# The time mix levels of an RWKV-7 layer: two halves of the chunks half a level apart

## The chip, the cores and the metric

The kernel runs on one core of one Trainium2 chip. It is one launch, and what counts is the device time of that launch in microseconds (us). The core has five engines that run their own instruction queues and meet at semaphores: PE (TensorE, matrix products), DVE (VectorE), ACT (ScalarE), POOL (GpSimd) and SP (SyncE). In the profile PEld stands for the weight loads of PE, which overlap its products. PE writes only to the eight PSUM banks; DVE and ACT read them from there.

## The reference, cut to what matters

The program is a whole model of several layers in float32 on 512 tokens of width 1024. Its first layer is an RWKV-7 time mix with 16 heads of width 64, a recurrence over the tokens:

```python
def rwkv7_time_mix(x, mu, w_rkv, ...):
    ...
    def step(S, inp):
        r_t, d_t, k_t, v_t, a_t, b_t = inp
        sa = jnp.einsum('bhij,bhj->bhi', S, a_t)
        S = (S * d_t[:, :, None, :] + sa[..., None] * b_t[:, :, None, :]
             + v_t[..., None] * k_t[:, :, None, :])
        return S, jnp.einsum('bhij,bhj->bhi', S, r_t)

    _, y = lax.scan(step, state0, tuple(seq_first(z) for z in (r_h, decay, k_h, v_h, vec_a, vec_b)))
    ...
```

What follows (group norm, gate, output product, feed-forward, attention layers, a second block) is not touched by the change and is left out here.

## The kernel before

The heads are taken in pairs (`PAIRS` = 8, index `n`), one head on the first 64 partitions and one on the last 64. The 512 tokens of a pair are cut into 8 chunks of 64. Inside a chunk the recurrence is a lower triangular system, and the kernel inverts its 64x64 matrix by doubling: from 2x2 blocks to 4x4 and so on, in five **levels** (`LEVELS` = 1 to 5). A pair goes through three parts:

1. the opening (`opening_tensor`, `opening_vector`): the products that make the matrices, into PSUM, and their masks. It ends on PE with three dense products of the next pair;
2. the levels (`levels_tensor`, `levels_vector`), which the change rewrites;
3. the scan over the eight chunks (`scan_tensor`, `scan_vector`), which needs the finished inverses, and in which one dense product of the next pair stands behind each short product that has to wait for DVE.

The chunks are in two groups, `g` = 0 (chunks 0 to 3) and `g` = 1 (4 to 7). In a level each chunk and head has three 64x64 products: T (`ga` times `xz[..., 0]`), which DVE multiplies by the mask of the level into `ti`; then X and Z (both with `ti` and `xz[..., 1]`), which DVE adds to `xz`. The last level has no X. `PLACES` says which quarter of the 128x128 array a product uses: T and X use the two quarters off the diagonal (from the rows of one head to the partitions of the other), Z the two on it. Products in different quarters run side by side. Each float32 product shows as two records in the trace.

A level on PE is: T of group 0, T of group 1, a fill, X and Z of group 0, X and Z of group 1, a fill. DVE masks group 0 and then 1, has a fill of its own, and adds group 0 and then 1. A **fill** is work of something else that is written between: on PE, by `in_level`, dense products of the next pair (`dense_tensor`, numbered 3 to 10; 3 to 7 are the last of the keys, at L476; 8 is two short products for w and a, at L491 and L492; 9 and 10 are r, at L498), `var_tensor` (L522) and `spread_tensor` (L530) of the group norm of the pair before; on DVE, by `in_levels`, the rest of that norm (`y_var` to `gated`, L1014 to L1037) and `sigmoid` (L867) of the next pair. In the last pair the fills on PE are output products (L697) instead. The first pair has no norm to finish.

All queues are strictly in the order in which the code writes them. PE waits for `level_dve` (steps of DVE), DVE for `level_pe`; each step is one increment of a semaphore.

Of the kernel before, what the change touches and what calls it, by code (L numbers as in the profile page):

```python
# [18 lines left out]
ALU = mybir.AluOpType  # L19
# [3 lines left out]
P = 128  # L23
T = 512
# [5 lines left out]
CH = 64  # L30
# [202 lines left out]
def refined(dve, v, r, done):  # L233
# [30 lines left out]
LEVEL_PE = ["low", "gram0", "gram1"] + [f"{w}{lv}_{g}" for lv in LEVELS for w in ("T", "XZ") for g in range(2)]  # L264
LEVEL_DVE = (["bonus", "low", "x_first", "gram_b0", "gram_b1", "gram_k0", "z_one0", "z_one1", "z_first", "gram_k1"]
             + [f"{w}{lv}_{g}" for lv in LEVELS for w in ("T", "XZ") for g in range(2)])
# [12 lines left out]
class TimeMix:  # L279
# [321 lines left out]
    def levels_tensor(self, pe, n, fill):  # L601

        ps, S, V = self.k.ps, self.level_pe, self.level_dve
        xz, ti = self.xz, self.ti

        for lv in LEVELS:
            for g in range(2):
                pe.wait_ge(V.sem, V.at(n, f"XZ{lv - 1}_{g}" if lv > 1 else f"gram_b{g}"))  # L610
                for c in range(4):
                    for rows, other in self.PLACES:
                        ins = pe.matmul(ps[other, 2 * g, 256 + c * CH:256 + c * CH + CH], self.ga[rows, 4 * g + c, 0:CH],
                                        xz[rows, g, 0, c, :], start=True, stop=True)
                S.done(ins, f"T{lv}_{g}")
            fill(lv, 0)
            for g in range(2):
                pe.wait_ge(V.sem, V.at(n, f"T{lv}_{g}"))
                if lv == 1 and g:
                    pe.wait_ge(self.turned_act.sem, self.turned_act.at(n, "K"))  # L620
                for c in range(4):
                    cols = slice(c * CH, c * CH + CH)
                    if lv < LEVELS[-1]:
                        for rows, other in self.PLACES:
                            pe.matmul(ps[rows, 2 * g, cols], xz[other, g, 1, c, :], ti[other, 4 * g + c, :], start=True, stop=True)
                    for rows, other in self.PLACES:
                        ins = pe.matmul(ps[other, 2 * g + 1, cols], ti[other, 4 * g + c, :], xz[other, g, 1, c, :], start=True,
                                        stop=True)
                S.done(ins, f"XZ{lv}_{g}")
            fill(lv, 1)  # L630
# [70 lines left out]
    def tensor(self, pe):  # L701
# [10 lines left out]
        in_level = {(1, 0): 1, (1, 1): 1, (2, 0): 1, (2, 1): 1, (3, 0): 1, (4, 1): 1, (5, 0): 2}  # L712
# [248 lines left out]
    def levels_vector(self, dve, n, fill):  # L961
        k, ps, S, V = self.k, self.k.ps, self.level_pe, self.level_dve
        levels = k.const(CR_AT, "levels")
        for lv in LEVELS:
            mask = levels[:, lv * CH:lv * CH + CH].unsqueeze(1).broadcast_to([P, 4, CH])
            for g in range(2):
                dve.wait_ge(S.sem, S.at(n, f"T{lv}_{g}"))
                V.done(dve.tensor_tensor(self.ti[:, 4 * g:4 * g + 4, :], ps[:, 2 * g, 256:512].rearrange("p (c t) -> p c t", c=4),
                                         mask, ALU.mult), f"T{lv}_{g}")
            fill(lv)  # L970
            for g in range(2):
                dve.wait_ge(S.sem, S.at(n, f"XZ{lv}_{g}"))
                if lv < LEVELS[-1]:
                    both = self.xz[:, g].rearrange("p w c t -> p w (c t)")
                    ins = dve.tensor_tensor(both, both, ps[:, 2 * g:2 * g + 2, 0:256], ALU.add)
                else:
                    z = self.xz[:, g, 1].rearrange("p c t -> p (c t)")
                    ins = dve.tensor_tensor(z, z, ps[:, 2 * g + 1, 0:256], ALU.add)
                V.done(ins, f"XZ{lv}_{g}")
# [2297 lines left out]
```

## Time and profile before

| | us |
|---|---|
| median of 3 runs | 2375.32 (2373.02 to 2380.53) |
| the profiled execution | 2380.81 |
| its span in the trace | 2379.0 |
| from the first weight load of the levels to the first of the scan, pair 2 | 21.91 |
| one whole pair (opening, levels, scan) | 60.68 |

The profile lists instructions by engine with start and length; "idle before" is how long the engine stood still, and behind the arrow stands who released it. A timeline merges neighbours of one line into one row (x32 is 32 records). The chain of work is followed back from the last instruction to what released each step. Mean granted clock of PE over the span is 0.98 of full speed, and 1.00 in the time mix up to the last pair's scan.

### The profile page before, as it was taken

The page shows a single profiled execution, that of the slowest core. Times are in us where ns is not written, and L with a number is a line of the kernel's source. Part 1 is how long each engine was busy: PE and PEld are TensorE (multiplying, and loading weights), DVE is VectorE, ACT ScalarE, POOL GpSimd, SP SyncE. Part 2 cuts the span into 40 slices and gives each one's busy share as a digit, 9 for nine tenths or more (in the row PEclk, how much of TensorE's full clock was granted, in tenths as well). Part 3 has the DMA queues.
Part 4 walks back from the last instruction along what each step waited for, and adds up shares of the span by engine and source line. Part 5 has one row for each costly group of instructions (what it writes and reads, how often), then busy time and mean ns, then how long its engine had stood idle before and what let it go on. Part 6 is the DMA issues. An engine that isn't in the chain of part 4 may idle for free.

```text
span 2379.0 us, 38698 instructions
## 1 busy us (share of the span) xinstructions
PE 2281.1 (96%) x15454; PEld 1526.7 (64%) x15454; DVE 1149.0 (48%) x2701; ACT 652.1 (27%) x1461; POOL 5.6 (0%) x9
## 2 busy tenths in 40 slices
PE   7999999998999999999999897999999998999998
PEld 3555555555788888865486776888845554444553
DVE  7455555552766662254336565632553564222542
ACT  2222222211333320145332222301221452113541
POOL 0000000000000000000000000000000000000000
PEclk9999999999999999999999999999899998999998
DMA  2100000002222222211113232222212110221111
GB/s 105 61 32 32 32 32 32 20 20 90 89 89 80 81 99 98 85 33 39 54 54 95 91 103 74 106 98 85 106 53 80 36 45 36 72 72 51 36 36 71
DMA packets 27123, 154.78 MB, mean 65 GB/s; under 512 B 5856, under 2 KB 5984, under 8 KB 13152
## 3 DMA queue, kind: packets, MB, share of 16 engines
q1 hardware_dynamic: 22032, 145.57, 17.1%
q0 software_dynamic: 4944, 7.10, 1.3%
q8 instruction: 110, 1.80, 0.3%
q14 instruction: 37, 0.30, 0.0%
HBM read 146.61 MB, written 6.03 MB: 64 GB/s over the span
## 4 chain that ended last, share of the span: by engine, by line
PE 88%; DMA 5%; DVE 5%; issue 1%; ACT 1%; DVEq 0%; SPq 0%; ACTq 0%
PE banks L1868 14%; PE banks L1329 11%; PE banks L1201 7%; PE banks L1129 6%; DMA arena<-up 5%; PE banks L2358 5%; PE banks L1248 3%; PE banks L2210 3%; PE banks L508 3%; PE banks L476 3%; PE banks L498 2%; PE banks L1171 2%; PE banks L1838 2%; PE banks L2244 2%; PE banks L2222 2%; PE banks L2955 2%
## 5 line engine op out<-in xcount | busy, mean ns | idle before, releaser
L1868 PE MATMUL banks<-arena 128*128 128x256 f32 x2016 | 443.0, 381 | 30.9 <-DMA arena<-up 25.9
L1868 PEld LDWEIGHTS banks<-arena 128*128 128x128 f32 x2016 | 383.5, 191 | 90.9 <-issue 36.4
L1329 PE MATMUL banks<-arena 128*128 128x256 f32 x1232 | 267.5, 378 | 0.0
L1329 PEld LDWEIGHTS banks<-arena 128*128 128x128 f32 x1232 | 232.3, 189 | 33.5
L1201 PE MATMUL banks<-arena 128*128 128x512 f32 x384 | 170.8, 602 | 0.0
L1923 ACT ACTIVATE arena<-banks 128x256 f32<-128x256 f32 x180 | 69.0, 384 | 282.8 <-PE banks L1868 282.8
L2083 DVE SCALAR_TENSOR_TENSOR arena<-arena 128x511 f32<-128x511 f32 (+1 forms) x144 | 108.2, 752 | 68.2 <-ACT arena L1932 51.0
L1129 PE MATMUL banks<-arena 128*128 128x512 f32 x320 | 141.1, 602 | 0.0
L2311 DVE CUSTOM_DVE_ANT_0 arena<-banks,arena 128x256 f32<-128x256 f32 (+3 forms) x160 | 70.8, 472 | 132.7 <-PE banks L2210 132.2
L2279 ACT ACTIVATE arena<-arena 128x128 f32<-128x128 f32 (+3 forms) x192 | 101.5, 530 | 121.9 <-DVE arena L2311 121.8
L2067 DVE TENSOR_TENSOR arena<-arena 128x512 f32<-128x512 f32 x144 | 97.3, 691 | 74.3 <-DMA arena<-up 57.9
L1201 PEld LDWEIGHTS banks<-arena 128*128 128x128 f32 x384 | 72.8, 192 | 93.5 <-issue 91.4
L2358 PE MATMUL banks<-arena 128*128 128x512 f32 x256 | 127.7, 627 | 3.0 <-DVE arena L1786 3.0
L1129 PEld LDWEIGHTS banks<-arena 128*128 128x128 f32 x320 | 61.3, 193 | 77.7 <-issue 77.7
L1447 DVE TENSOR_TENSOR arena<-arena 128x1408 f32<-128x1408 f32 x32 | 51.6, 1625 | 104.8 <-DMA arena<-down 82.3
L2210 PE MATMUL banks<-arena 64*128 64x256 f32 (+7 forms) x384 | 93.7, 451 | 0.9 <-DVE arena L2311 0.9
L2222 PEld LDWEIGHTS banks<-arena 128*128 128x128 f32 x392 | 47.4, 144 | 62.3 <-issue 33.5
L1248 PE MATMUL banks<-arena 128*128 128x256 f32 x384 | 85.8, 379 | 0.0
L2358 PEld LDWEIGHTS banks<-arena 128*128 128x128 f32 x256 | 45.2, 193 | 58.8 <-issue 53.7
L1248 PEld LDWEIGHTS banks<-arena 128*128 128x128 f32 x384 | 71.6, 189 | 9.8
L2222 PE MATMUL banks<-arena 128*128 128x128 f32 x392 | 62.0, 283 | 12.2 <-DVE arena L2328 6.8
L1932 ACT ACTIVATE arena<-arena 128x512 f32<-128x512 f32 x72 | 58.2, 811 | 48.8 <-DVE arena L2075 48.8
(324 smaller groups left out, 3186.3 us busy)
## 6 DMA issues: line engine op xcount, KB each, us to landing
arena<-up SPq DMA_DIRECT2D x44, 1024.0 KB, 4.8
arena<-down SPq DMA_DIRECT2D x16, 1408.0 KB, 6.1
arena<-w_mix SPq DMA_DIRECT2D x8, 1728.0 KB, 7.0
arena<-e_in SPq DMA_DIRECT2D x12, 1024.0 KB, 4.8
arena<-o_in SPq DMA_DIRECT2D x8, 1024.0 KB, 4.8
arena<-w_o SPq DMA_DIRECT2D x4, 1024.0 KB, 4.9
arena<-q SPq DMA_DIRECT2D x8, 512.0 KB, 3.4
arena<-o_attn SPq DMA_DIRECT2D x4, 1024.0 KB, 4.8
```

Of the source, the lines that this page charges most:

```text
L476: ins = pe.matmul(ps[:, 4, :], w(8 + j), self.xk[:, j, :], start=j == 0, stop=j == 7)
L1129: ins = pe.matmul(k.ps[:, j, :], k.ring[s][:, (m * kt + t) * P:(m * kt + t + 1) * P], source[:, t, :], start=t == 0, stop=t == kt - 1)
L1201: ins = pe.matmul(k.ps[:, j % 4, :], ring[:, (m * KT + t) * P:(m * KT + t + 1) * P], k.h[:, t, :], start=t == 0, stop=t == KT - 1)
L1248: return pe.matmul(k.ps[:, first_bank + 2 * s + m, half], k.ring[s][:, (m * KT + t) * P:(m * KT + t + 1) * P], bridge.xg[n][:, t, half], s ...
L1329: ins = pe.matmul(ps[:, bank, LO], w[:, t, :], x[:, t, :], start=first and t == 0, stop=t == last, skip_group_check=not first)
L1868: ins = pe.matmul(out, w[:, q, :], x[:, q, :], start=start and q == 0, stop=q == 3, skip_group_check=not start)
L2067: W.done(dve.tensor_tensor(self.s[name], x, y, op), name)
L2083: dve.scalar_tensor_tensor(conv[m][:, shift:T], self.row[m][:, 0:T - shift], self.k.vec("conv", col + tap), conv[m][:, shift:T], ALU.mult, ...
L2210: self.scored.done(pe.matmul(self.k.ps[:, w, 0:k1 - k0], part.query(n, w, b), part.key(n, w, k0, k1), start=True, stop=True), "x")
L2222: ins = pe.transpose(self.k.ps[:, bank, o:o + P], p[:, i * P:i * P + P], self.ident)
L2279: self.exped.done(act.activation(p, raw, ACT.Exp, bias=self.col("max", c, w), scale=-1.0, accum_out=self.col("sum", c, w)), "x")
L2358: ins = pe.matmul(k.ps[:, 6 + n % 2, :], k.ring[slot][:, t * P:t * P + P], k.h[:, t, :], start=t == 0, stop=t == KT - 1)
```

## The change

Three things are done, all in the levels.

**The stretches.** Before the first level PE computes T of group 0 alone (`first`). Then each level has a stretch A: T of group 1 together with Z and X of group 0, chunk by chunk; a fill; and a stretch B: T of group 0 for the next level together with Z and X of group 1; a fill. One step of `level_pe` is signalled at the end of each stretch, where before each group had its own. DVE does, behind A, the mask of group 1 and the sum of group 0, and behind B, the mask of group 0 for the next level and the sum of group 1. In the last level there is no X, and B has Z alone.

**The fills on PE.** `in_level` had one dense product at each of (1,0), (1,1), (2,0), (2,1), (3,0), (4,1) and two at (5,0). Now there is one at each of (1,1), (2,0), (2,1), (3,0), (4,0), (4,1), (5,0), (5,1). The sum stays 8. `var_tensor` stays at (1,0) and `spread_tensor` at (3,1).

**The fills on DVE.** `y_var`, `y_inverse`, `y_r0` go from level 1 to 2, and `y_r1` to `y_r3` from 2 to 3.

```diff
-            for g in range(2):
-                pe.wait_ge(V.sem, V.at(n, f"XZ{lv - 1}_{g}" if lv > 1 else f"gram_b{g}"))
-                for c in range(4):
-                    for rows, other in self.PLACES:
-                        ins = pe.matmul(ps[other, 2 * g, 256 + c * CH:256 + c * CH + CH], self.ga[rows, 4 * g + c, 0:CH],
-                                        xz[rows, g, 0, c, :], start=True, stop=True)
-                S.done(ins, f"T{lv}_{g}")
+            pe.wait_ge(V.sem, V.at(n, f"T{lv}_0"))
+            pe.wait_ge(V.sem, V.at(n, f"XZ{lv - 1}_1" if lv > 1 else "gram_b1"))
+            for c in range(4):
+                below(1, c)
+                ins = inverse(lv, 0, c)
+            S.done(ins, f"A{lv}")
             fill(lv, 0)
...
+            pe.wait_ge(V.sem, V.at(n, f"XZ{lv}_0"))
+            if lv == 1:
+                pe.wait_ge(self.turned_act.sem, self.turned_act.at(n, "K"))
+            for c in range(4):
+                if lv < LEVELS[-1]:
+                    below(0, c)
+                ins = inverse(lv, 1, c)
+            S.done(ins, f"B{lv}")
             fill(lv, 1)
...
-        in_level = {(1, 0): 1, (1, 1): 1, (2, 0): 1, (2, 1): 1, (3, 0): 1, (4, 1): 1, (5, 0): 2}
+        in_level = {(1, 1): 1, (2, 0): 1, (2, 1): 1, (3, 0): 1, (4, 0): 1, (4, 1): 1, (5, 0): 1, (5, 1): 1}
...
+        dve.wait_ge(S.sem, S.at(n, "first"))
+        masked(1, 0)
         for lv in LEVELS:
...
+            dve.wait_ge(S.sem, S.at(n, f"A{lv}"))
+            masked(lv, 1)
+            added(lv, 0)
             fill(lv)
...
+            dve.wait_ge(S.sem, S.at(n, f"B{lv}"))
+            if lv < LEVELS[-1]:
+                masked(lv + 1, 0)
+            added(lv, 1)
...
-        in_levels = {1: ["y_var", "y_inverse", "y_r0"], 2: ["y_r1", "y_r2", "y_r3"], 4: ["normed"], 5: ["biased", "gated"]}
+        in_levels = {2: ["y_var", "y_inverse", "y_r0"], 3: ["y_r1", "y_r2", "y_r3"], 4: ["normed"], 5: ["biased", "gated"]}
```

`below` is the product T and `inverse` the products Z and X, with the same operands as before.

PE, first pair, from the last dense product of the opening on. Before (L613 is T, L625 is X, L627 is Z, L476 a dense product):

```order
L476 MATMUL banks<-arena 128x512 x2
L613 MATMUL banks<-arena 64x64 [waits mix_level_dve]
L613 MATMUL banks<-arena 64x64 x7
L613 MATMUL banks<-arena 64x64 [waits mix_level_dve]
L613 MATMUL banks<-arena 64x64 x7
L476 MATMUL banks<-arena 128x512
L625 MATMUL banks<-arena 64x64 [waits mix_level_dve]
L625 MATMUL banks<-arena 64x64
L627 MATMUL banks<-arena 64x64 x2
```

And in the changed kernel (L611 is T, L618 is Z, L621 is X):

```order
L476 MATMUL banks<-arena 128x512 x2
L611 MATMUL banks<-arena 64x64 [waits mix_level_dve]
L611 MATMUL banks<-arena 64x64 x7
L611 MATMUL banks<-arena 64x64 [waits mix_level_dve]
L611 MATMUL banks<-arena 64x64
L618 MATMUL banks<-arena 64x64 x2
L621 MATMUL banks<-arena 64x64 x2
L611 MATMUL banks<-arena 64x64 x2
L618 MATMUL banks<-arena 64x64 x2
L621 MATMUL banks<-arena 64x64 x2
```

Each half level before had two waits, one for each group, and a dense product behind T; now a stretch has one wait at its start, nothing stands between `first` and A1, and T of one group alternates with Z and X of the other.

DVE, first pair, in the levels. Before (L968 the mask, L975 and L978 the sum, L867 `sigmoid`):

```order
L968 TENSOR_TENSOR arena<-banks,arena 128x256 [waits mix_level_pe] x2
L975 TENSOR_TENSOR arena<-arena,banks 128x512 [waits mix_level_pe] x2
L968 TENSOR_TENSOR arena<-banks,arena 128x256 [waits mix_level_pe] x2
L867 TENSOR_SCALAR arena<-arena 128x512 [waits mix_early_act]
L978 TENSOR_TENSOR arena<-arena,banks 128x256 [waits mix_level_pe] x2
```

And in the changed kernel, the last two levels (L981 the mask, L987 and L990 the sum, L881 `sigmoid`):

```order
L981 TENSOR_TENSOR arena<-banks,arena 128x256 [waits mix_level_pe]
L987 TENSOR_TENSOR arena<-arena,banks 128x512
L981 TENSOR_TENSOR arena<-banks,arena 128x256 [waits mix_level_pe]
L990 TENSOR_TENSOR arena<-arena,banks 128x256
L881 TENSOR_SCALAR arena<-arena 128x512 [waits mix_early_act]
L990 TENSOR_TENSOR arena<-arena,banks 128x256 [waits mix_level_pe]
```

Each DVE instruction of the levels waited for PE before; now one wait stands ahead of a mask and a sum.

## Rows read from the trace of the kernel before

**Rows 1.** The page: busy time by engine, with its share of the span.
```profile
PE 2281.1 (96%) x15454; PEld 1526.7 (64%) x15454; DVE 1149.0 (48%) x2701; ACT 652.1 (27%) x1461; POOL 5.6 (0%) x9
```

**Rows 2.** The chain in order of time (start us, length us, what): pairs 1 and 2.
```profile
141.77 2.78 PE banks L476 x6
...
202.45 2.78 PE banks L476 x6
```

**Rows 3.** Busy time of each engine (us) in the levels of pairs 0, 2 and 7.
```profile
85.29:105.71 20.42, 19.49 (x467) 12.79 (x466) 10.66 (x22) 4.55 (x6) 0.00 (x0) 1.00 0.21 82
...
205.16:227.07 21.91, 21.22 (x491) 14.40 (x490) 13.43 (x31) 4.81 (x7) 0.00 (x0) 1.00 0.20 78
505.95:527.74 21.79, 21.14 (x495) 14.37 (x492) 15.22 (x34) 1.08 (x3) 0.00 (x0) 1.00 0.15 51
```

The columns behind the stretch are its length, then PE, PEld, DVE, ACT and POOL with their records, the granted clock, the DMA share and GB/s.

**Rows 4.** Timeline of PE (start, length, what), pair 2, levels 1 to 3.
```profile
206.24 1.05 PE L522 MATMUL banks<-arena 128*128 128x2 f32 x8
...
210.33 1.15 PE L613 MATMUL banks<-arena 64*64 64x64 f32 x32
211.41 1.12 PE L476 MATMUL banks<-arena 128*128 128x512 f32 x2
212.47 0.27 PE L625 MATMUL banks<-arena 64*64 64x64 f32 x2
...
214.62 1.15 PE L613 MATMUL banks<-arena 64*64 64x64 f32 x32
```

**Rows 5.** Timeline of DVE, pair 2, level 2.
```profile
211.06 0.89 DVE L968 TENSOR_TENSOR arena<-banks,arena 128x256 f32<-128x256 f32 x2 [0.83 <-PE banks L613]
...
213.23 1.28 DVE L975 TENSOR_TENSOR arena<-arena,banks 128x512 f32<-128x512 f32 x2 [0.79 <-PE banks L627]
```

**Rows 6.** Timeline of the weight loads, pair 2, levels 4 and 5 and the scan's first.
```profile
218.86 1.01 PEld L613 LDWEIGHTS banks<-arena 64*64 64x64 f32 x32 [0.17 <-DVE arena L975]
220.07 0.14 PEld L625 LDWEIGHTS banks<-arena 64*64 64x64 f32 x2 [0.20 <-DVE arena L968]
...
222.34 1.01 PEld L613 LDWEIGHTS banks<-arena 64*64 64x64 f32 x32 [0.76 <-DVE arena L975]
...
225.34 0.78 PEld L627 LDWEIGHTS banks<-arena 64*64 64x64 f32 x24 [0.76 <-issue]
...
227.07 0.22 PEld L640 LDWEIGHTS banks<-arena 64*64 64x64 f32 x4 [0.72 <-issue]
```

**Rows 7.** Timeline of DVE, pair 2, levels 4 and 5.
```profile
219.60 0.89 DVE L968 TENSOR_TENSOR arena<-banks,arena 128x256 f32<-128x256 f32 x2 [0.80 <-PE banks L613]
220.40 0.74 DVE L1031 SCALAR_TENSOR_TENSOR arena<-arena,banks 128x512 f32<-128x512 f32 x1
221.06 1.28 DVE L975 TENSOR_TENSOR arena<-arena,banks 128x512 f32<-128x512 f32 x2
...
223.88 0.74 DVE L1034 SCALAR_TENSOR_TENSOR arena<-arena 128x512 f32<-128x512 f32 x1
224.66 0.69 DVE L1037 TENSOR_TENSOR arena<-arena 128x512 f32<-128x512 f32 x1
225.27 0.42 DVE L867 TENSOR_SCALAR arena<-arena 128x512 f32<-128x512 f32 x1
226.07 0.89 DVE L978 TENSOR_TENSOR arena<-arena,banks 128x256 f32<-128x256 f32 x2 [0.38 <-PE banks L627]
```

**Rows 8.** Groups of instructions by line (busy us, mean ns, idle before): sum and mask.
```profile
L975 DVE TENSOR_TENSOR arena<-arena,banks 128x512 f32<-128x512 f32 x64 | 41.1, 685 | 23.8 <-PE banks L627 23.8
...
L968 DVE TENSOR_TENSOR arena<-banks,arena 128x256 f32<-128x256 f32 x80 | 33.9, 425 | 33.8 <-PE banks L613 32.2
```

**Rows 9.** The chain: eight and two dense products in a row.
```profile
65.33 6.88 PE banks L508 x16
...
102.14 1.91 PE banks L498 x4
```

**Rows 10.** Timeline of ACT, pair 2: w of the next pair.
```profile
222.42 0.69 ACT L768 ACTIVATE arena<-banks,arena 128x512 f32<-128x512 f32 x1 [3.08 <-PE banks L492]
```

More of the change, by code:

```diff
@@ L263 @@
              "b", "b_grown", "a_decayed", "rk", "r_decayed"]
[L264 removed]
+LEVEL_PE = ["low", "gram0", "gram1", "first"] + [f"{w}{lv}" for lv in LEVELS for w in "AB"]
 LEVEL_DVE = (["bonus", "low", "x_first", "gram_b0", "gram_b1", "gram_k0", "z_one0", "z_one1", "z_first", "gram_k1"]
[L266 removed]
+             + ["T1_0"] + [x for lv in LEVELS for x in (f"T{lv}_1", f"XZ{lv}_0") + (f"T{lv + 1}_0",) * (lv < 5) + (f"XZ{lv}_1",)])
 SCAN_PE = [f"{w}{c}" for c in range(NC) for w in (("rhs", "u", "side", "state", "y") if c < NC - 1 else ("rhs", "u", "side", "y"))]
@@ new lines, in below, with inverse @@
+        def below(g, c):
+            for rows, other in self.PLACES:
+                ins = pe.matmul(ps[other, 2 * g, 256 + c * CH:256 + c * CH + CH], self.ga[rows, 4 * g + c, 0:CH],
+                                xz[rows, g, 0, c, :], start=True, stop=True)
+            return ins
+        def inverse(lv, g, c):
+            cols = slice(c * CH, c * CH + CH)
+            for rows, other in self.PLACES:
+                ins = pe.matmul(ps[other, 2 * g + 1, cols], ti[other, 4 * g + c, :], xz[other, g, 1, c, :], start=True, stop=True)
+            if lv < LEVELS[-1]:
+                for rows, other in self.PLACES:
+                    ins = pe.matmul(ps[rows, 2 * g, cols], xz[other, g, 1, c, :], ti[other, 4 * g + c, :], start=True, stop=True)
+            return ins
@@ new lines, in levels_tensor @@
+        pe.wait_ge(V.sem, V.at(n, "gram_b0"))
+        for c in range(4):
+            ins = below(0, c)
+        S.done(ins, "first")
+        for lv in LEVELS:
+            pe.wait_ge(V.sem, V.at(n, f"T{lv}_0"))
[4 more added lines that the diff above has]
+            S.done(ins, f"A{lv}")
+            fill(lv, 0)
+            pe.wait_ge(V.sem, V.at(n, f"XZ{lv}_0"))
+            if lv == 1:
+                pe.wait_ge(self.turned_act.sem, self.turned_act.at(n, "K"))
+            for c in range(4):
+                if lv < LEVELS[-1]:
+                    below(0, c)
+                ins = inverse(lv, 1, c)
+            S.done(ins, f"B{lv}")
@@ L963, in levels_vector, with masked, added @@
         levels = k.const(CR_AT, "levels")
-        for lv in LEVELS:
[L965 to L969, printed above, removed]
-            fill(lv)
[L971 to L979, printed above, removed]
+        def masked(lv, g):
+            mask = levels[:, lv * CH:lv * CH + CH].unsqueeze(1).broadcast_to([P, 4, CH])
+            V.done(dve.tensor_tensor(self.ti[:, 4 * g:4 * g + 4, :], ps[:, 2 * g, 256:512].rearrange("p (c t) -> p c t", c=4),
+                                     mask, ALU.mult), f"T{lv}_{g}")
+        def added(lv, g):
+            if lv < LEVELS[-1]:
+                both = self.xz[:, g].rearrange("p w c t -> p w (c t)")
+                ins = dve.tensor_tensor(both, both, ps[:, 2 * g:2 * g + 2, 0:256], ALU.add)
+            else:
+                z = self.xz[:, g, 1].rearrange("p c t -> p (c t)")
+                ins = dve.tensor_tensor(z, z, ps[:, 2 * g + 1, 0:256], ALU.add)
+            V.done(ins, f"XZ{lv}_{g}")
+        dve.wait_ge(S.sem, S.at(n, "first"))
+        masked(1, 0)
+        for lv in LEVELS:
+            dve.wait_ge(S.sem, S.at(n, f"A{lv}"))
+            masked(lv, 1)
+            added(lv, 0)
+            fill(lv)
+            dve.wait_ge(S.sem, S.at(n, f"B{lv}"))
+            if lv < LEVELS[-1]:
+                masked(lv + 1, 0)
+            added(lv, 1)
     def scan_vector(self, dve, n, fill):
```

13 lines of the change are left out of this document (removed).

## The prediction, made before the changed kernel ran

> **What bounds the kernel now.** I read the page first, then the busy time by stretch, then the timelines of PE and DVE through one pair. PE is busy for 96% of the span and DVE for 48% [rows 1], so the question is only how long PE takes for a pair and where it stands still. The chain passes the same point of the opening every 60.68 us [rows 2], and 21.91 us of that are the levels; PE is busy in 21.22 of these [rows 3]. A pair has thus under 1 us of idle PE in its levels, at a granted clock of 1.00, the 2.4 GHz level. That is all that a better order could win without taking work away, some 5.5 us in eight pairs.
>
> How a level hides DVE today is seen in level 2. T takes PE 1.08 us (210.33 to 211.41), the dense product 1.06 us (to 212.47), and X and Z with the next dense product 2.15 us (to 214.62) [rows 4]. DVE starts on the first group 0.73 us after T began [rows 5], long before PE is through with the second group. So what PE needs first, group 0, is made while PE computes group 1. Where no dense product stands between, this shows: in level 4 T begins at 218.86 and X and Z at 220.07, 1.21 us later, after the mask of group 0 alone; PE is idle for about 0.13 us [rows 6]. The other wait is at the end: the last Z begins at 225.34 and the scan at 227.07, 1.73 us for 1.08 us of products [rows 6].
>
> **The round trip of a stretch.** The change signals once per stretch, at its end, and lets DVE do a mask and a sum before PE may start the next stretch, which needs both. The terms:
> - From the start of a stretch to DVE's first instruction. With half of the products it is 0.73 us for T and 0.76 us for X and Z [rows 4, 5]. The second of two masks ends 0.89 us after the first began and takes 0.425 us [rows 5, 8], so it began 0.47 us after the first: it too waited for PE, whose second half takes that long. A whole stretch therefore wakes DVE after 1.20 to 1.23 us. I take 1.22.
> - Mask and sum. Two DVE instructions with no wait between overlap by 0.08 us: L1031 takes 0.74 us, and the next starts 0.66 us behind it [rows 7]. So 0.425 - 0.08 + 0.685 [rows 8] = 1.03 us.
> - From DVE's end to PE's weight load: 219.60 + 0.425 = 220.02, and the load is at 220.07 [rows 6, 7]: 0.05 us.
>
> Together 2.30 us, with a bound of 2.28 below. PE's own work in the same time is 1.09 for the stretch and 1.06 for the dense product, 2.15 us at most [rows 4]; with w and a as the fill 2.27 (220.07 to 222.34) [rows 6]. The round trip ends last in every stretch, by 0.15 us where a dense product fills it. That a mixed stretch is no longer than one of X and Z rests on the quarters: X and Z put 8 products in each of four quarters; T of one group with X and Z of the other puts 8 into the two off the diagonal and 4 into the two on it. No row shows the alternating order. If the swaps of the two off-diagonal quarters cost something, I allow 0 to 0.06 us per stretch, the upper end being about one record's spacing (1.08 us by 16 records in each of two quarters is 0.07) [rows 4]; I take 0, since the order of X and Z with its four quarters costs no more than that of T with two. The bound above is thus 2.36 us.
>
> **A pair, part by part.**
> 1. `first` to A1. Nothing stands between. Half a T wakes DVE after 0.73, the mask takes 0.425, the release 0.05: 1.21 us, of which PE works 0.61. This is the same 1.21 us that level 4 shows now [rows 6].
> 2. A1 to A5 are eight intervals. In a middle pair A1 has the norm's sums as its fill (L522, at most 1.05 us [rows 4]), B3 its spread; both are shorter than the round trip allows. 8 x 2.30 = 18.40 us.
> 3. A5 and B5 have 4 products per quarter, 0.61 us each. On PE: 0.61 + 1.06 (product 9) + 0.61 + 1.06 (product 10) = 3.34 us to the scan. On DVE: 0.75 to wake, 0.34 mask, 0.34 sum of Z (an L978 takes as long as a mask: two of either in 0.89 us [rows 7]), then its fill: `biased` 0.78, `gated` 0.61, `sigmoid` 0.34 [rows 7], and only then the last sum, 0.42 and 0.05 to the scan: 3.63 us. DVE ends last. The wait for w that `sigmoid` has is met: product 8 is ready a whole stretch earlier, and ACT needs 0.69 us [rows 10].
>
> A middle pair: 1.21 + 18.40 + 3.63 = 23.24 us against 21.91, **+1.33 us**, six times: +8.0. The first pair has no norm, so PE ends last: 1.21 + 18.40 + 3.34 = 22.95 us against 20.42 [rows 3]: +2.5; it gains least from the fills, since A1 and B3 now stand bare. The last pair has no `sigmoid`: DVE 3.29, PE 3.34, so 22.95 us against 21.79: +1.2. **Sum: +11.7 us**; with 2.28 us it is 10.4, with 2.36 it is 15.5 (64 intervals).
>
> What the change saves is in there: X, Z and T share stretches, so PE has 0.3 us less of tile work in a pair (10 x 1.085 = 10.85 against 3 x 0.61 + 8 x 1.09 = 10.55), and the late half of level 5 has cover. It is lost to the wait for DVE. The steps of the norm that move on DVE (`y_var` and on) cost nothing: DVE has 2.30 - 1.03 = 1.27 us free in each interval, and they are six short ones. Product 3 moves behind the norm's sums and product 7 a half level on; ACT's copy of the key starts later, and its next reader, product 9, stands two stretches behind. The scan and the opening keep their order, and no DMA issue is moved.
>
> **A rule on the drain.** Eight dense products in a row take 6.88 us, two 1.91 [rows 9], one 1.06 [rows 4]: 0.86 each, and 0.2 per run. The change has two more runs in a middle pair (9 and 10 apart; 3 parted from L522). The Trainium skill (TensorEngine Tiling (Array Packing), Key Properties) says that a change of tiling mode drains the engine, and speaks against such a change; the trace agrees with 0.2 us. By that rule alone the change would cost 0.4 us a pair, some 3 us; by my sum this lies under the round trip and costs nothing of its own.
>
> **Rivals.** (a) The round trip stays hidden and PE sets the pace. It decides where the trip falls to 2.15 us, 0.15 less than my rows give; mask and sum would have to overlap far more than 0.08 us, or DVE wake earlier. Then a middle pair is 1.21 + 8 x 2.15 + 3.34 = 21.75, -0.16; the first pair 21.75, +1.3; the last -0.05; the sum is 0.3 us: 2375.6, not slower. Against it: 1.28 us for two sums and 0.89 for two masks are the same in all eight pairs. Even this best case is no gain, because the start of the levels is bare. For over 0.3% faster each pair would have to lose 0.9 us, all of its idle time. (b) The diagonal quarters don't run beside the alternating pair, so that a stretch has 12 slots in place of 8: +0.47 us each, in 64 intervals +30 us: 2417. It speaks against it that X and Z share the array in 1.09 us. (c) The change doesn't do what it says: what is late is not the round trip but the DVE fill in level 5 alone; then each pair is near (a) plus 0.3 us, 2378. It needs the same short trip as (a).
>
> **How the numbers follow.** The profiled execution of before took 2380.8 us, 5.5 over the median of 2375.3; the levels are all at clock 1.00, so the difference of 11.7 carries over: 2392.5 for an execution like that one, and for the median 2375.3 + 11.7 = **2387.0**. My sum has 0.76; (a) and (c) together 0.17; (b) 0.04; something faster 0.03. The runs of before spread by 3 to 5 us, so the sum's own 2385.7 to 2390.8 becomes 2382 to 2394; I let the lower end reach to 2380 for a part of (c). Under 0.3% (7.1 us) this kernel's measurement can't tell a difference from none: 2368.2 to 2382.4 is "same". Faster 0.04, same 0.20, slower 0.76.
>
> **What would show it.** In the changed profile: starts of stretches 2.28 to 2.36 us apart in all pairs, each released by the DVE sum; DVE's mask 1.2 us behind a stretch's start; 1.21 us from `first` to A1; 3.6 us from A5 to the scan, with L881 just ahead of the last sum; the pair's period 62.0 us in place of 60.68. Wrong would be: stretches 2.15 apart with PE never idle (rival a), a stretch of products longer than 1.15 us (b), or a scan or opening that has changed its length.

## The result

| | us |
|---|---|
| the changed kernel, median of 4 runs | 2398.02 (2391.92 to 2406.84) |
| before, beside it, 4 runs | 2374.17 (2369.88 to 2380.53) |
| ratio, with its 95% interval | 1.0094 (1.0065 to 1.0123) |
| the profiled execution; its span | 2397.51; 2395.7 |

The change made the kernel slower, as forecast, but by about twice the forecast: 22 us or so instead of 11.7, and the median of 2398.0 us lies above the range of 2380 to 2394.

**Where it went.** The page of the changed kernel, as [rows 1]:

```profile
PE 2282.1 (95%) x15454; PEld 1524.5 (64%) x15454; DVE 1144.8 (48%) x2701; ACT 651.2 (27%) x1461; POOL 5.6 (0%) x9
```

The same work is done, and PE stands still for longer. The levels of pairs 2, 3 and 7, and a piece of pair 7, in busy time by stretch, as [rows 3] (length, then PE, PEld, DVE, ACT, POOL, the granted clock, DMA share, GB/s):

```profile
210.61:234.10 23.49, 21.64 (x491) 14.06 (x490) 12.87 (x31) 4.81 (x7) 0.00 (x0) 1.00 0.18 71
272.92:298.91 25.99, 21.91 (x491) 14.16 (x490) 12.88 (x31) 4.81 (x7) 0.00 (x0) 1.00 0.16 63
522.58:549.99 27.41, 24.53 (x496) 16.34 (x493) 14.81 (x34) 1.18 (x3) 0.00 (x0) 0.88 0.12 41
526.60:533.40 6.80, 6.80 (x96) 5.16 (x100) 2.04 (x4) 0.27 (x1) 0.00 (x0) 0.50 0.07 12
```

From the first product of the levels to that of the scan, pair by pair (us):

| pair | 0 | 1 | 2 | 3 | 4 | 5 | 6 | 7 |
|---|---|---|---|---|---|---|---|---|
| before | 20.42 | 21.92 | 21.91 | 21.92 | 21.92 | 21.92 | 21.92 | 21.85 |
| forecast | 22.95 | 23.24 | 23.24 | 23.24 | 23.24 | 23.24 | 23.24 | 22.95 |
| after | 23.66 | 23.79 | 23.49 | 25.99 | 23.80 | 24.00 | 23.49 | 27.40 |

The scan (31.3 us up to the next opening) is as long as before, and the opening too, both within 0.1 us. The levels together take 21.9 us more, and the stretch from the first levels to the end of the time mix 498.7 us instead of 476.5. Pairs 2 and 6 show the plain pattern. It is the forecast one; here are the weight loads that begin `first`'s successor A1 (211.82), its fill, and B1, A2 and B2, each with what released it, as [rows 6] (the rows are from three stretches of that timeline):

```profile
211.82 0.14 PEld L611 LDWEIGHTS banks<-arena 64*64 64x64 f32 x2 [0.67 <-DVE arena L981]
212.90 0.97 PEld L522 LDWEIGHTS banks<-arena 128*128 128x128 f32 x8
214.10 0.14 PEld L611 LDWEIGHTS banks<-arena 64*64 64x64 f32 x2 [0.23 <-DVE arena L987]
...
216.44 0.17 PEld L611 LDWEIGHTS banks<-arena 64*64 64x64 f32 x2 [0.96 <-DVE arena L987]
...
218.75 0.14 PEld L611 LDWEIGHTS banks<-arena 64*64 64x64 f32 x2 [0.90 <-DVE arena L987]
```

And DVE beside them, as [rows 5]:

```profile
213.03 0.42 DVE L981 TENSOR_TENSOR arena<-banks,arena 128x256 f32<-128x256 f32 x1 [1.26 <-PE banks L621]
213.37 0.68 DVE L987 TENSOR_TENSOR arena<-arena,banks 128x512 f32<-128x512 f32 x1
215.30 0.43 DVE L981 TENSOR_TENSOR arena<-banks,arena 128x256 f32<-128x256 f32 x1 [1.26 <-PE banks L621]
215.65 0.68 DVE L987 TENSOR_TENSOR arena<-arena,banks 128x512 f32<-128x512 f32 x1
217.68 0.42 DVE L981 TENSOR_TENSOR arena<-banks,arena 128x256 f32<-128x256 f32 x1 [1.35 <-PE banks L621]
```

A1 begins at 211.82, DVE's mask at 213.03 (1.21 us later), its sum at 213.37 (0.34 later) and ends at 214.05, and B1 begins at 214.10. That is the round trip of the forecast: 2.28 us. The stretch A1 itself takes 1.08 us (to L522 at 212.90), so T beside Z and X in alternation costs the array nothing. From B1 to A2 it is 2.34 us: the sum ends at 216.33 and PE's load is at 216.44, 0.11 us later in place of 0.05. The intervals alternate, 2.34 and 2.31, from there on.

Pair 3 has something else. In its timeline of weight loads A1 and B1 are as in pair 2, and then, inside B1 (the third row; the fourth begins A2):

```profile
274.13 0.14 PEld L611 LDWEIGHTS banks<-arena 64*64 64x64 f32 x2 [0.67 <-DVE arena L981]
276.41 0.14 PEld L611 LDWEIGHTS banks<-arena 64*64 64x64 f32 x2 [0.23 <-DVE arena L987]
279.05 0.13 PEld L621 LDWEIGHTS banks<-arena 64*64 64x64 f32 x1 [2.10 <-issue]
280.96 0.17 PEld L611 LDWEIGHTS banks<-arena 64*64 64x64 f32 x2 [0.94 <-DVE arena L987]
```

PE stops for 2.1 us in the middle of a run of products, with no semaphore to wait for. The DMA queues between 272 and 279 us (packets, MB, share of the 16 engines) show what moves at that time: a slab of the next weights (1.7 MB in one load), and one packet of instructions, which starts at 276.67 us, behind most of the slab.

```profile
q1 hardware_dynamic: 144, 1.77, 71.7%
q8 instruction: 1, 0.02, 0.8%
```

Pairs 0, 1, 4 and 5 have such pauses of 0.3 to 0.5 us, all in A2, and pair 3 has one more of 0.3 us ahead of A3. And in pair 7 A1 begins 2.82 us after `first`, not 1.21, and the clock then falls to half, the 1.2 GHz level, for 6.8 us (the last row of the stretches above). The first loads of A1 in that pair:

```profile
525.40 0.14 PEld L611 LDWEIGHTS banks<-arena 64*64 64x64 f32 x2 [2.27 <-DVE arena L981]
```

And DVE ahead of them, which is still at the last of the opening's masks (L948) 1 us after the end of `first` (523.27), and comes to the mask of the levels (L981) only then:

```profile
524.33 0.69 DVE L948 TENSOR_TENSOR arena<-banks,arena 128x512 f32<-128x512 f32 x1
524.93 0.41 DVE L981 TENSOR_TENSOR arena<-banks,arena 128x256 f32<-128x256 f32 x1
```

So the first trace divides the 21.9 us: 11.7 as forecast; 1.9 for the longer hand-over (23.49 for 23.24 in six pairs, 0.2 in each of the other two); 4.1 in pauses (0.5, 0.3, 2.5, 0.3 and 0.5 in pairs 0, 1, 3, 4 and 5); 1.6 for the bare start of pair 7; 2.6 for the half clock (intervals of 2.83, 3.91 and 2.83 for 2.28, 2.34 and 2.31). Whether the last three belong to the change or to one execution was open. Behind the time mix this trace is 5.8 us shorter than that of before (1811.4 for 1817.2 us, with 72 and 83 us of half clock there). The work there is the same in all kernels; the twelve traces of this document have 1805 to 1815 us for it in the seven with the new stretches, and 1817 in four of the five with the old ones (1809 in the fifth, e6). Why the clock falls less there in some executions was not tested. So the length of the time mix is the better measure of the change, and most ratios of the kernels with the new stretches come out somewhat lower than their time mixes do.

### The profile page after: what moved, and what is told of

It is laid out like the page before. It is cut to its first block, busy times and chain, and to the rows that moved or that the text cites. A ratio compares the mean times of both kernels' runs of the same rounds, so it can differ in the third digit from the quotient of the medians.

```text
span 2395.7 us, 38738 instructions
## 1 busy us (share of the span) xinstructions
PE 2282.1 (95%) x15454; PEld 1524.5 (64%) x15454; DVE 1144.8 (48%) x2701; ACT 651.2 (27%) x1461; POOL 5.6 (0%) x9
## 4 chain that ended last, share of the span: by engine, by line
PE 84%; DVE 8%; DMA 6%; issue 2%; ACT 1%; DVEq 0%; SPq 0%; ACTq 0%
PE banks L1892 14%; PE banks L1353 11%; PE banks L1225 7%; PE banks L1153 6%; DMA arena<-up 5%; PE banks L2382 5%; PE banks L1272 3%; PE banks L2234 3%; PE banks L508 3%; PE banks L1862 2%; PE banks L1195 2%; PE banks L611 2%; PE banks L2268 2%; PE banks L498 2%; PE banks L2246 2%
## 5 line engine op out<-in xcount | busy, mean ns | idle before, releaser
L1892 PEld LDWEIGHTS banks<-arena 128*128 128x128 f32 x2016 | 384.3, 191 | 90.4 <-issue 35.4
L1353 PEld LDWEIGHTS banks<-arena 128*128 128x128 f32 x1232 | 232.2, 189 | 33.6
L1225 PEld LDWEIGHTS banks<-arena 128*128 128x128 f32 x384 | 72.5, 192 | 92.9 <-issue 90.9
L1153 PEld LDWEIGHTS banks<-arena 128*128 128x128 f32 x320 | 60.4, 190 | 76.4 <-issue 76.4
L611 PEld LDWEIGHTS banks<-arena 64*64 64x64 f32 x1280 | 63.7, 136 | 65.3 <-DVE arena L987 52.4
L611 PE MATMUL banks<-arena 64*64 64x64 f32 x1280 | 78.4, 225 | 17.1 <-DVE arena L987 8.5
L2246 PEld LDWEIGHTS banks<-arena 128*128 128x128 f32 x392 | 48.3, 146 | 62.3 <-issue 33.5
L2382 PEld LDWEIGHTS banks<-arena 128*128 128x128 f32 x256 | 44.7, 191 | 58.1 <-issue 52.9
L981 DVE TENSOR_TENSOR arena<-banks,arena 128x256 f32<-128x256 f32 x80 | 34.0, 425 | 93.0 <-PE banks L621 78.8
```

The costliest lines, as they stand in the source:

```text
L1153: ins = pe.matmul(k.ps[:, j, :], k.ring[s][:, (m * kt + t) * P:(m * kt + t + 1) * P], source[:, t, :], start=t == 0, stop=t == kt - 1)
L1225: ins = pe.matmul(k.ps[:, j % 4, :], ring[:, (m * KT + t) * P:(m * KT + t + 1) * P], k.h[:, t, :], start=t == 0, stop=t == KT - 1)
L1353: ins = pe.matmul(ps[:, bank, LO], w[:, t, :], x[:, t, :], start=first and t == 0, stop=t == last, skip_group_check=not first)
L1892: ins = pe.matmul(out, w[:, q, :], x[:, q, :], start=start and q == 0, stop=q == 3, skip_group_check=not start)
L2246: ins = pe.transpose(self.k.ps[:, bank, o:o + P], p[:, i * P:i * P + P], self.ident)
L2382: ins = pe.matmul(k.ps[:, 6 + n % 2, :], k.ring[slot][:, t * P:t * P + P], k.h[:, t, :], start=t == 0, stop=t == KT - 1)
```

## The experiments

Each was timed beside the kernel before. The time mix in the tables is that from the first product of the first levels to the first output product behind the time mix, in the trace.

### e1: the changed kernel again

No edit.

> The changed kernel itself, once more, for a second trace and a narrower ratio. In its first trace the levels took 21.9 us more than before: some 12 by round trips that were forecast and 2 more by their release, 4.1 by pauses of PE inside a stretch in five pairs (0.3 to 2.5 us, behind the weights' load of the next pair but one), 1.6 by the bare start of the last pair and 2.6 by a half clock in it. Theory: all of these have places in the program and return, in the same pairs within 0.5 us; the ratio is 1.008 to 1.011. Rival: the pauses and the clock are accidents of one execution; then they are gone or elsewhere, and the ratio is near 1.006.

Measured: 1.0083 (1.0058 to 1.0107), median 2397.68 against 2379.64 us. Pairs 2, 3, 7 and the whole time mix:

```profile
210.12:233.59 23.47, 21.64 (x491) 14.06 (x490) 12.87 (x31) 4.81 (x7) 0.00 (x0) 1.00 0.18 71
272.45:299.36 26.91, 23.27 (x491) 14.80 (x490) 12.87 (x31) 4.81 (x7) 0.00 (x0) 0.94 0.16 62
523.46:550.83 27.37, 24.52 (x496) 16.32 (x492) 14.79 (x34) 1.18 (x3) 0.00 (x0) 0.88 0.12 41
...
85.90:585.08 499.18, 462.59 (x7651) 274.05 (x7650) 236.67 (x606) 99.30 (x184) 0.00 (x0) 0.98 0.08 27
```

The pauses return in pairs 3 (2.24 us), 4 (0.35) and 5 (1.0), hardly in 1 (0.1) and not in 0. Pair 3's is again inside B1 at the same instruction's line:

```profile
278.59 0.18 PEld L621 LDWEIGHTS banks<-arena 64*64 64x64 f32 x1 [2.10 <-issue]
```

The half clock of pair 7 returns at 527.5 us, again 6.8 us long, and there is one more, of 3.4 us from 278.3 on, at the pause of pair 3. That half clock begins 0.3 us before the pause ends. So most of the places are the program's, and the sizes differ from execution to execution. The time mix is 22.7 us longer than before. The theory holds in the main: the bare start of pair 7 and its half clock return, and so do the pauses of pairs 3, 4 and 5; the one of pair 0 does not, and pair 3 is 0.9 us longer than in the first trace, more than the 0.5 us that I allowed.

### e2: the slab of weights is asked for later

```diff
-                if j == 0 and n:
-                    k.begun(ins, slot)
...
-                if n == 0 and t == 0:
+                if (n == 0 and t == 0) or (n and t == 2):
                     k.begun(ins, slot)
```

> The changed kernel with one edit: the step that lets the next slab of weights (1.7 MB) be loaded is signalled by a product in the scan, not by the first of the three products ahead of the levels. Theory: PE's pauses in the first stretches are fetches of its own instructions (16 KB each) that come behind that slab's packets; then the pauses of 0.3 to 2.5 us are gone from the levels, each middle pair takes 23.5 us there, and the kernel is some 4 us faster than the changed one, a ratio of 1.006 to 1.009 to before. Rival: the pauses have to do with the stretches themselves (the alternating quarters, or the semaphores); then nothing moves.

Measured: 1.0070 (1.0045 to 1.0096), median 2393.23 us, 4.5 less than e1. Pairs 2, 3 and the time mix:

```profile
210.75:235.55 24.80, 23.12 (x491) 14.79 (x491) 12.87 (x31) 4.80 (x7) 0.00 (x0) 0.93 0.01 3
274.38:297.87 23.49, 21.64 (x491) 14.06 (x490) 12.87 (x31) 4.80 (x7) 0.00 (x0) 1.00 0.02 3
86.59:582.03 495.44, 461.78 (x7651) 273.41 (x7650) 236.67 (x606) 99.10 (x184) 0.00 (x0) 0.98 0.08 28
```

With no slab on its way in the levels (DMA share 0.02 for 0.16) pair 3 takes 23.49 us, and so do pairs 1, 4, 5 and 6, to 0.01 us. No pause is left anywhere. Pair 2 is 1.3 us longer, which is a half clock of 3.4 us at 214.6. So the slab's place is the cause. That it acts through PE's own instruction fetch rests on the timing: in the first trace and e1's each pause of A2 or B1 ends 2.2 to 2.6 us after a fetch of 16 KB had begun inside the slab's transfer, and where the fetch had begun ahead of the slab (pair 3 in e5, below), there was none. No run moved a fetch alone. The queue q8 is PE's by its count: in the first trace it brings, from the levels of pair 1 to those of pair 6, 39 packets of 16 KB for 9960 records of PE, some 64 bytes a record, and DVE and ACT together have 620. A fetch inside the slab does not always stop PE: the trace of before has one in pair 1 (at 148.54) and one in pair 5 (at 391.46), and no pause. The 0.3 us ahead of A3 in pair 3 of the first trace comes 3.9 us after a fetch, when the slab has landed; what it is stays open.

### e3: mask and sum waited for apart

```diff
             pe.wait_ge(V.sem, V.at(n, f"T{lv}_0"))
+            for c in range(4):
+                inverse(lv, 0, c)
             pe.wait_ge(V.sem, V.at(n, f"XZ{lv - 1}_1" if lv > 1 else "gram_b1"))
             for c in range(4):
-                below(1, c)
-                ins = inverse(lv, 0, c)
+                ins = below(1, c)
...
-            pe.wait_ge(V.sem, V.at(n, f"XZ{lv}_0"))
+            pe.wait_ge(V.sem, V.at(n, f"T{lv}_1"))
...
+            for c in range(4):
+                ins = inverse(lv, 1, c)
+            if lv < LEVELS[-1]:
+                pe.wait_ge(V.sem, V.at(n, f"XZ{lv}_0"))
+                for c in range(4):
+                    ins = below(0, c)
```

> The changed kernel with the work of a stretch in two parts, each behind its own wait: first Z and X, which need the mask alone, then T, which needs the sum. Same products, same fills, same instructions on DVE. Theory: what costs is that a stretch waits for mask and sum together; now the mask alone is on the path (1.22 + 0.42 + 0.05 = 1.7 us), which product and dense product cover, so filled stretches come 2.15 us apart in place of 2.33, a middle pair takes 22.2 to 22.5 us and the kernel is 10 to 14 us faster than the changed one, 1.002 to 1.006 of before. Rival: the alternating order or the drains of the array set 2.33; then the stretches stay at 2.3 us.

Measured: 1.0033 (1.0015 to 1.0050), median 2387.61 us, 10 less than e1; time mix 486.47 us, 12.7 less. Starts of stretches in pair 2 (L618 is Z, L476 the dense product), and the pair as a whole:

```profile
213.06 0.14 PEld L618 LDWEIGHTS banks<-arena 64*64 64x64 f32 x2 [0.76 <-DVE arena L984]
214.15 0.30 PEld L476 LDWEIGHTS banks<-arena 128*128 128x128 f32 x2
215.20 0.14 PEld L618 LDWEIGHTS banks<-arena 64*64 64x64 f32 x2 [0.76 <-DVE arena L984]
216.30 0.30 PEld L476 LDWEIGHTS banks<-arena 128*128 128x128 f32 x2
217.35 0.14 PEld L618 LDWEIGHTS banks<-arena 64*64 64x64 f32 x2 [0.76 <-DVE arena L984]
```
```profile
207.62:229.86 22.24, 21.47 (x491) 14.32 (x490) 12.88 (x31) 4.81 (x7) 0.00 (x0) 1.00 0.19 76
```

2.15 us from stretch to stretch instead of 2.33, with the same products and DVE instructions: the wait for the sum at a stretch's head is what cost. The edit also ends the alternation of T with Z and X, but that had cost nothing, as the stretch of 1.08 us in the first trace shows. A middle pair is then 22.24 us, still 0.3 us over before. Pair 7's half clock of 6.8 us is there again; pauses stand in pairs 1 (0.65 us) and 5 (1.07 us) alone. In e1 they came to 3.7 us, and there was a half clock in pair 3, so of the 12.7 us some 2.5 are not the edit's; by the pairs without a pause it is worth 1.25 us in a middle pair, 1.8 in the first and 1.0 in the last, 10.3 us together.

### e4: the list of fills alone

The kernel before, with this edit:

```diff
-        in_level = {(1, 0): 1, (1, 1): 1, (2, 0): 1, (2, 1): 1, (3, 0): 1, (4, 1): 1, (5, 0): 2}
+        in_level = {(1, 1): 1, (2, 0): 1, (2, 1): 1, (3, 0): 1, (4, 0): 1, (4, 1): 1, (5, 0): 1, (5, 1): 1}
```

> The kernel before with the changed kernel's list of fills on PE alone (one product each at (1,1), (2,0), (2,1), (3,0), (4,0), (4,1), (5,0), (5,1)); the stretches are as before. Theory: the list is the good part of the change: the wait of level 4 and the one ahead of the scan get a product, T of level 1 has the norm's sums for cover; a middle pair takes 21.4 to 21.6 us in the levels in place of 21.91, the kernel is 3 to 5 us faster than before (0.998). Rival: the split of products 9 and 10 and of 3 from the norm's sums costs its drains (0.2 us each) and eats it: the same time as before within 1 us, or slower.

Measured: 0.9985 (0.9965 to 1.0005), median 2374.83 against 2379.64 us. Pairs 3 and 7 and the time mix:

```profile
264.17:285.47 21.30, 21.30 (x492) 14.37 (x491) 13.25 (x31) 4.81 (x7) 0.00 (x0) 1.00 0.19 77
501.63:523.66 22.03, 21.42 (x497) 14.42 (x493) 15.16 (x34) 1.03 (x3) 0.00 (x0) 1.00 0.14 51
85.14:557.67 472.53, 455.30 (x7651) 273.05 (x7650) 239.75 (x606) 99.42 (x184) 0.00 (x0) 0.99 0.08 29
```

In pair 3 PE is busy in all of 21.30 us; before it was 21.22 of 21.92. The two extra runs of dense products cost less than the waits they cover. The trace shows the gain (4.0 us); the ratio alone leaves it open, since the interval takes in 1. Pair 7 loses 0.2 us. It has no product at (1,0) now, but e6 puts one there and takes 0.3 us longer still, so the reason is not shown.

### e5: cover for the start of the last pair

The changed kernel, with this edit:

```diff
         S.done(ins, "first")
+        fill(0, 1)
...
-                last_fill(in_level.get((lv, half), 0))
+                last_fill(3 if lv == 0 else in_level.get((lv, half), 0))
```

> The changed kernel with one edit: in the last pair alone three output products stand between the first T and stretch A1, where PE waited 2.3 us for DVE's opening; they are missing from the last slots of its scan. Theory: that bare wait is what let the granted clock fall to half in this pair's levels in both traces so far (at 526.6 and 527.5 us, 6.8 us long, the 1.2 GHz level), so without it the clock stays at 1.00, the pair's levels take 23.7 to 24.5 us in place of 27.4 and the kernel is 2 to 3 us faster than the changed one. Rival: the fall comes from the stretches as such, or from the lack of the three dense products of the opening; then there is a half clock in this pair again and its levels take 26 us or more.

Measured: 1.0055 (1.0037 to 1.0072), median 2390.07 us. Pair 7's levels:

```profile
520.43:545.76 25.33, 24.26 (x502) 15.12 (x498) 14.94 (x34) 1.18 (x3) 0.00 (x0) 1.00 0.13 45
```

The clock is 1.00 in this pair and stays so until 568.9 us. The levels are longer than I expected (25.3 for at most 24.5 us) because the three products themselves now stand in them: they take 2.8 us where the wait was 2.2, so A1 begins 3.39 us after `first`. They are missing in the scan. From the pair's first T to the end of the time mix it is 58.3 us for 61.8. The time mix is 6.0 us shorter than in the first trace; the other 2.5 are the pause of pair 3, which this trace does not have: there the fetch began at 271.7, ahead of the slab.

### e6: the parts that pay, together

The kernel before with e4's list, e2's edit, and one output product at (1,0) in the last pair.

```diff
-                last_fill(in_level.get((lv, half), 0))
+                last_fill(1 if (lv, half) == (1, 0) else in_level.get((lv, half), 0))
```

> The kernel before with the new list of fills (as e4), the late signal for the slab (as e2), and in the last pair one output product at (1,0). Theory: levels of 19.96 us in the first pair, 21.30 in all middle ones with no pause, 21.4 in the last: 4.6 us less than before in all, a ratio of 0.998. Rival: the late slab makes the weights late in the next pair, or the single products cost more elsewhere; then the scan or the opening are longer than 31.33 and 7.43 us.

Measured: 0.9960 (0.9944 to 0.9975), median 2369.00 against 2380.11 us. Pair 3 and the time mix:

```profile
265.02:286.32 21.30, 21.30 (x492) 14.37 (x491) 13.26 (x31) 4.81 (x7) 0.00 (x0) 1.00 0.01 3
86.18:558.60 472.42, 455.49 (x7652) 273.24 (x7651) 239.78 (x606) 99.28 (x184) 0.00 (x0) 0.99 0.09 29
```

19.97 us in the first pair and 21.29 or 21.30 in all middle ones, as expected; 22.3 in the last, 0.9 more than I expected. The time mix is 4.1 us shorter than before. This beats both kernels, though the ratio says more than the trace: 9.5 us for 4.1. The runs e9 and e10 ask why.

### e7: the new stretches with the old list

The changed kernel, with e4's diff the other way round.

> The changed kernel's stretches with the list of fills of the kernel before. Theory: the round trip of 2.33 us holds wherever one product or none is in a stretch, A1 with the norm's sums and a product takes 3.05 us, A5 with two products 2.5, the scan waits bare for DVE: a middle pair takes 24.1 to 24.3 us in the levels against 23.49, so the kernel is 4 to 6 us slower than the changed one, 1.010 to 1.013 of before. Rival: the new list itself has a part in the loss; then this one is no slower than the changed one.

Measured: 1.0087 (1.0056 to 1.0118), median 2399.34 us. Pair 2 and the time mix:

```profile
211.27:235.64 24.37, 21.28 (x491) 14.07 (x491) 12.96 (x31) 4.81 (x7) 0.00 (x0) 1.00 0.17 70
84.83:588.40 503.57, 458.52 (x7651) 273.05 (x7650) 237.34 (x606) 99.23 (x184) 0.00 (x0) 0.99 0.08 27
```

The time mix is 27.1 us over before and 4.4 to 4.9 over the changed kernel, so the trace bears the theory out. The ratio lies below the expected 1.010 to 1.013, and the four times can't tell this kernel from the changed one. In both schedules the new list is worth some 4 to 5 us by the time mix; the pauses hide a part of it here, since they come to 4 us in the first trace of the changed kernel and to about 1 us in this one. The loss is the stretches'.

### e8: three causes taken away

The changed kernel with the edits of e2, e3 and e5.

> The changed kernel with three causes taken away at once: the parts of a stretch wait apart (e3), the slab is signalled late (e2), and the last pair has three output products ahead of A1 (e5). Theory: the causes are separate and add up: 21.35 us in the first pair, 22.24 in the middle ones with no pause, 22.5 to 23.5 in the last, no half clock before the end of the time mix: 3 to 5 us over before, a ratio of 1.001 to 1.002. Rival: part of the loss is something else that the stretches bring and that no edit has touched; then the ratio stays at 1.003 or above.

Measured: 1.0011 (0.9992 to 1.0029), median 2378.19 against 2380.11 us. Pairs 2 and 7 and the time mix:

```profile
206.22:228.45 22.23, 21.46 (x491) 14.32 (x490) 12.87 (x31) 4.81 (x7) 0.00 (x0) 1.00 0.02 3
509.11:533.26 24.15, 24.15 (x503) 15.44 (x499) 14.64 (x34) 0.88 (x3) 0.00 (x0) 1.00 0.14 47
85.12:566.20 481.08, 457.34 (x7652) 274.01 (x7651) 236.70 (x606) 99.37 (x184) 0.00 (x0) 0.99 0.08 29
```

Of the 22.2 us that the time mix had gained in length, 4.6 are left, and the times are those of before within their interval. Every middle pair takes 22.24 us, no pair has a pause, and there is no half clock before 556.3 us, in the last products of the last scan. The last pair is 24.15 us, for it holds the three products. The causes add up: 10.3 us of e3's own, 4.1 of pauses and 3.5 in the last pair (e5) are 17.9, and 17.6 are gone; nothing larger is hidden. The 0.3 us that a middle pair still has over before lie at its end. There DVE does its fill ahead of the last sum (L992), as in the forecast, and the scan can't begin (167.45 us) before that sum ends:

```profile
165.98 0.69 DVE L1063 TENSOR_TENSOR arena<-arena 128x512 f32<-128x512 f32 x1
166.59 0.42 DVE L883 TENSOR_SCALAR arena<-arena 128x512 f32<-128x512 f32 x1
166.92 0.42 DVE L992 TENSOR_TENSOR arena<-arena,banks 128x256 f32<-128x256 f32 x1
```

### e9 and e10: is the late slab worth something by itself

e9 is the kernel before with e2's edit; e10 is e6 once more.

> The kernel before with the late signal for the slab alone. e6 measured 0.996, but its trace has the time mix only 4.1 us shorter, as e4's, which measured 0.9985; this run asks whether the late slab has a part of its own. Theory: PE makes no pause in the levels of before, so there is nothing to win: time mix of 476.5 us in the trace, a ratio of 1.000 within 0.2%. Rival: the late slab wins something that the first trace doesn't show (the time behind the time mix, or pauses in other executions); then the ratio is 0.998 or below.

> e6 once more, on the chip of e9. Theory: the time mix again takes 472.4 us, and the ratio lies between those of e4 and e6, near 0.998. Rival: 0.996 is what the kernel is worth, and a part of it lies behind the time mix.

Measured: e9 1.0007 (0.9987 to 1.0028), e10 0.9971 (0.9951 to 0.9990). The time mix of e9:

```profile
85.63:562.98 477.35, 455.17 (x7652) 274.30 (x7651) 240.90 (x606) 99.24 (x184) 0.00 (x0) 0.99 0.08 29
```

The late slab gives nothing where PE makes no pause. e10's time mix is 473.1 us, its levels equal to e6's within 0.02 us, and its span differs from e6's by 8.8 us, of which 8.5 lie behind the time mix (1817.1 for 1808.6 us, with 83 and 70 us of half clock). That part varies from one execution to the next. What e6 is worth by its trace is 4 us, 0.17%; the two ratios, 0.996 and 0.997, hold that only just (0.9983 is inside e10's interval and outside e6's).

The executions themselves explain a good part of the rest. Each has its mean granted clock listed, from 0.978 to 0.987, and the time follows it: those of before that were timed beside e6 take 2382.4 us at 0.979 and 2371.5 at 0.986. Comparing each execution with the mean of those of before at the same figure gives this:

| kernel | us against before at the same clock | executions |
|---|---|---|
| e4 | -4.1 | 12 |
| e9 | -0.6 | 12 |
| e6, e10 | -5.6, -5.8 | 11, 12 |
| e1 (the changed kernel), e7 | +17.1, +23.2 | 6, 4 |

So e4's gain of 4 us is in the times too, and e7 is 6 us slower than the changed kernel, as its trace says. e6 and e10 are worth some 5.7 us, about 2 more than their traces say, and why is open; the other 4 us or so of e6's ratio are executions that happened to have the higher clock. (For kernels with a half clock of their own, as e1 and e7, the comparison takes that out; it serves to set these two beside each other.)

## Why the prediction was right or wrong

**What failed, in one view.** The terms of the sum make 11.7 of the 21.9 us by which the levels grew. The other 10.2 are a term taken from a middle pair and used in the last one (1.6 us), the clock taken as unchanged (2.6), the instruction fetch put at nothing without a reason (4.1), and the hand-over a little too short (1.9). The first three are steps that failed; the last is a size.

**The direction and the mechanism of the stretches: right.** The round trip set the pace, and its terms held: 1.21 us to DVE's mask (I took 1.22), 1.02 us for mask and sum (I took 1.03), 0.05 us of release ahead of stretch B. `first` to A1 took 1.21 us in seven pairs. e3 took the sum off the head of the stretch and the intervals fell to 2.15 us, which is the value of PE's own work in the forecast.

**The hand-over: a small miss.** Ahead of stretch A the load comes 0.11 us after the sum, not 0.05, and so does the scan's first. In the trace a wait of 0.05 us stands there as an instruction of its own (at 216.36, L630), since the code waits for two steps. The row for it was there: in [rows 6, 7] L978 ends at 226.07 + 0.89 = 226.96 and the scan loads at 227.07. I took the shorter of two rows for all places. Together with 0.03 us more to DVE's mask from A2 on (216.44 to 217.68, 1.24 us) it cost 1.9 us: 2.34 and 2.31 in turn for my 2.30, and the end of level 5 3.71 for 3.63. It lay inside my bound of 2.36.

**The last pair: a step that failed.** I wrote that `first` to A1 "is the same 1.21 us that level 4 shows now" and used it in all eight pairs. In the last pair the opening has no dense products of a next pair, so PE reaches `first` 2.8 us sooner while DVE is still at the opening's masks: A1 waits for the opening's masks and begins 2.82 us after `first`. The cover that a change needs has to be looked up in the first and the last turn too, not in a middle one.

**"The levels are all at clock 1.00, so the difference carries over": wrong.** This took the clock as given, although the change makes PE stand still longer. The five traces in which the last pair has its bare wait (after, e1, e2, e3, e7) all have a half clock of 6.8 us in that pair's levels, which begins between the end of the wait and 1.7 us behind it; the seven in which it is covered or doesn't arise (before, e4, e5, e6, e8, e9, e10) have none there. The cost in the first trace is 2.6 us. What shows that the wait is the cause is e5, which fills it with three products from the scan and changes nothing else. The Trainium skill (TensorE: Matmul & The Clock Gate, HAM oscillation) says that gaps in which PE idles make the gate fall back to the half clock. The trace agrees in kind, and with a shorter gap than those it describes: 2.1 us between the end of `first` (523.3) and A1 (525.4), and the half clock from 526.6 on.

**Nothing on the instruction fetch: a missing cost.** No term of mine had PE's own instructions in it, and no row of before shows a pause. e2 shows that 3 to 4 us of the loss come from the slab's transfer (the edit brought 3.3 to 3.7 us in the time mix), and the timing points to fetches behind it. Why the new order has pauses and the old one none is argued, not shown: its first dense product comes 4.6 us into the levels of pair 2 (215.18), the old one's 2.0 us (207.15), so PE goes through its many small products sooner, while the slab is under way. The Trainium skill (Runtime: NRT & Kernel Launch, Instruction fetch mechanics) says that each engine refills its instructions in blocks of 16 KB by its own DMA queue; these traces agree, with the 39 packets of 16 KB on q8. It also says that straight code hides the fetch; the 2.1 us of "issue" in pair 3 speak against that.

**The drain rule.** That the drain speaks against the change was my own conclusion from the rule. By the rule alone the new list would have cost 3 us; e4 shows it gaining 4. The price of a run of its own is real (1.06 us for one product alone, 0.86 in a row), but the waits that the products cover were larger, as my sum had it.

**The rivals.** (a) and (c), the hidden round trip, are out by the intervals of 2.28 to 2.34 us; (b), the array, by a stretch of 1.08 us. The statement that even the best case of this order is no gain is borne out by e8, as far as it goes: with the wait for the sum off the head a middle pair takes 22.24 us where before has 21.92 and rival (a) had 21.75.

## What to carry to other kernels

When each of two half steps waits for the whole of the other's answer, every instruction of the answer is on the path; wait for each part where its reader stands (e3: 0.18 us of 2.33 in each of 64 intervals), and count the waits at the head. Before trusting an interval from the middle of a loop, look at the first and last turn, where the neighbours that give cover are missing, and at what else PE must have: its instructions, if a large load runs at the same time, and its clock, which fell in all five traces whose last pair had its start uncovered. A list of fills can be right where the schedule around it is wrong; test the two apart.

## What the runs showed of the hardware

- PE can stop for 0.3 to 2.2 us in the middle of a run of products, 2.2 to 2.6 us after a 16 KB fetch of its instructions began during a 1.7 MB load; the profile calls it "issue". In the three traces with the same middle pairs (after, e1, e5) it comes in pairs 4 and 5 every time, in pair 3 twice, in pairs 0 and 1 in some, with sizes that vary, and it is gone when the load is moved into the scan.
- A bare wait of 2.0 to 2.5 us between the weight loads of two stretches of small products was followed in five traces of five by 6.8 us at half clock. Two more half clocks of 3.4 us stand in levels: in pair 3 of e1, from within its pause of 2.1 us on, and in pair 2 of e2, where nothing had kept the weight loads waiting for more than 0.8 us. What sets these off was not tested.
- Small products of one group alternate with those of another in the quarters of the array at no cost: 24 products in 1.08 us, as long as the 16 of a T before, which use two quarters [rows 4].
